# Weights of a seven-product projection: requested in another queue, split in another order

## The reference

```python
h = rms_norm(x, norm_w[l]) * (1.0 + scale[:, None, :]) + shift[:, None, :]
proj = jnp.einsum('bsd,de->bse', h, w_in[l])                      # 2888 columns
u_pool, g_pool, q, k, v, g_attn, qi, ki, wi = jnp.split(proj, split_points, axis=-1)
pool_out = pool_mixer(u_pool, w_pool[l], pool_scale[l]) * jax.nn.silu(g_pool)
q = rope(rms_norm(q.reshape(B, S, N_HEADS, HEAD_DIM), q_norm_w[l]), pos)
k = rope(rms_norm(k.reshape(B, S, N_KV_HEADS, HEAD_DIM), k_norm_w[l]), pos)
qi, ki = rope(qi...), rope(ki...)
```

## Time and profile before

| | us |
|---|---|
| median of three executions | 3118.74 (3116.83 to 3121.08) |
| the profiled execution's own time | 3112.07 |
| its span, from the first to the last instruction | 3110.3 |
| TensorE busy | 2921.1 (94%) |
| VectorE busy | 2345.5 (75%) |
| ScalarE busy | 1748.3 (56%) |
| GpSimd busy | 349.3 (11%) |
| mean granted clock of TensorE | 0.975 of full speed |

### The profile page before, as it was taken

How to read it: one execution, slowest core, us unless ns; L and a number is a source line. 1 busy time by engine, 2 the same in 40 slices (tenths; PEclk the granted TensorE clock), 3 DMA queues, 4 the chain that set the end, 5 groups by cost and what they waited for, 6 DMA issues and landing times. The chain is left out here.

```text
span 3110.3 us, 49557 instructions
## 1 busy us (share of the span) xinstructions
PE 2921.1 (94%) x17248; PEld 2331.0 (75%) x17248; DVE 2345.5 (75%) x3555; ACT 1748.3 (56%) x3207; POOL 349.3 (11%) x695
## 2 busy tenths in 40 slices
PE   7999999999999999999999998798777899999899
PEld 5888888888878877777777777577656667777687
DVE  8888887766576859888879766666568898888553
ACT  5343422232455537777767654455378899888510
POOL 2000000000000441000100000000012333233100
PEclk8999999999999999999999999999988999999999
DMA  4434422257855883210137665566661111111774
GB/s 123 123 105 130 149 68 68 68 183 263 223 150 182 272 276 88 52 32 29 46 116 225 194 189 170 187 177 186 183 140 45 25 32 29 25 39 39 166 219 140
DMA packets 449820, 401.00 MB, mean 129 GB/s; under 512 B 106563, under 2 KB 379971, under 8 KB 447141
## 3 DMA queue, kind: packets, MB, share of 16 engines
q1 hardware_dynamic: 447764, 393.58, 43.1%
q0 software_dynamic: 1088, 3.93, 0.6%
q10 hardware_dynamic: 720, 0.31, 0.1%
HBM read 263.20 MB, written 124.49 MB: 125 GB/s over the span
## 5 line engine op out<-in xcount | busy, mean ns | idle before, releaser
L349 ACT ACTIVATE s_mx_w_hi<-s_mx_raw 128x512 fp32r<-128x512 f32 x224 | 138.5, 628 | 309.3 <-PE p_oa_acc L705 238.1
L705 PE MATMUL p_oa_acc<-s_h_a_hi,s_mx_w_hi 128*128 128x512 f32 x744 | 291.6, 392 | 8.4 <-DVE s_h_a_lo L448 7.1
L705 PE MATMUL p_oa_acc<-s_h_a_hi,s_mx_w_lo 128*128 128x512 f32 x744 | 290.5, 390 | 0.0
L705 PE MATMUL p_oa_acc<-s_h_a_lo,s_mx_w_hi 128*128 128x512 f32 x744 | 290.4, 390 | 0.0
L2143 PE MATMUL p_pr_ps<-s_pr_x_hi,s_pr_w_hi 128*128 128x512 f32 x588 | 235.0, 400 | 34.4 <-ACT s_pr_first L2137 18.0
L1862 DVE TENSOR_TENSOR_SCAN s_st_prod<-s_st_soft,s_st_prod 128x512 f32<-128x512 f32 x192 | 234.9, 1270 | 8.3 <-ACT s_st_soft L1789 7.6
L2143 PE MATMUL p_pr_ps<-s_pr_x_lo,s_pr_w_hi 128*128 128x512 f32 x588 | 232.4, 395 | 0.0
L2143 PE MATMUL p_pr_ps<-s_pr_x_hi,s_pr_w_lo 128*128 128x512 f32 x588 | 232.0, 395 | 0.0
L1789 ACT ACTIVATE s_st_soft<-p_st_z 128x512 f32<-128x512 f32 (+3 forms) x320 | 153.5, 532 | 109.4 <-PE p_st_z L1915 108.5
L4313 PE MATMUL p_sa_turn<-s_ident,s_sa_arg 128*128 128x128 f32 x1088 | 165.1, 287 | 40.5 <-ACT s_sa_prob L3911 22.3
L2108 DVE TENSOR_TENSOR s_pr_w_lo<-s_pr_w_raw,s_pr_w_hi 128x512 fp32r<-128x512 f32 x154 | 105.1, 687 | 119.2 <-ACT s_pr_w_hi L2103 118.9
(11 more groups left out here) (487 smaller groups left out, 7748.8 us busy)
## 6 DMA issues: line engine op xcount, KB each, us to landing
s_mx_raw<-in_w_in_a SPq DMA_DIRECT2D x128, 256.0 KB, 3.7
s_pr_w_raw<-d_w_sums SPq DMA_DIRECT2D x88, 256.0 KB, 3.7
s_pr_w_raw<-in_w_in SPq DMA_DIRECT2D x66, 256.0 KB, 3.7
s_pb_ada<-in_w_ada SPq DMA_DIRECT2D x16, 768.0 KB, 7.3
s_pb_block<-in_w_in SPq DMA_DIRECT2D x44, 256.0 KB, 4.6
d_w_sums<-s_pb_block SPq DMA_DIRECT2D x44, 256.0 KB, 3.0
d_rot_hi<-s_pr_rot SPq DMA_DIRECT2D x18, 512.0 KB, 2.9
d_y_t<-s_mx_y SPq DMA_DIRECT2D x16, 512.0 KB, 5.5
```

Of the source, the lines that this page charges most:

```text
L349: nc.scalar.activation(w_hi[:, m], raw[g % 2][:, m], ACT.Copy).then_inc(hi_done, 1)
L705: ins = nc.tensor.matmul(bank, w[:, m, k, :], a[:, m, k, :], start=(k == 0 and n == 0), stop=(k == KH - 1 and n == 2))
```

## The change

- SyncE no longer requests weights in this stage. All its loads of weights move to GpSimd's queue, in the order in which the products free the slots. Of group 0 (the tail) and group 1 they stand in `out_b_programs.gpsimd`, of the others in `rotate_programs.gpsimd`, where `late_difference` follows the loads of the tail 12.
- SyncE's loop keeps the swaps and the stores. `store_inverse` and `spread_inverse` come earlier in it, `load_ahead` moves from before group 11 to the end of group 10, `load_late_half(0)` goes behind the swap, and `load_first_rows` and `load_first_keys` go later.
- ScalarE makes the high part of a slot about two products after the same slot was freed: A12_B21, S3_T3, S4_B22 and A22_T4 within their own group, A11_B11, S1_T1 and S2_T2 (behind `keep_u3`) in the group before. `take_high` of the norm group g - 2 comes right behind `leave`, ahead of everything else.
- VectorE's order follows: `times_inverse` first, then `low_squares` or `add_windows`, `times_sin`, the low part of A12_B21, `times_cos`, `add_turned`, S3_T3, `low_turned` of the norm group, and so on. `leave_b` now stands ahead of `low_pooled`. `leave_b` of the tail 0 moves ahead of the last splits of the stage before (`leave_tail`).

```diff
@@ -2335,26 +2335,7 @@
                 load_x(n + 2)
-            if n == RESIDENT:
-                for h in range(2):
-                    pairs.load_tail(sp, 0, h)
             if RESIDENT <= n - 4:
                 store_late(n - 4)
-            if n == TILES - 2:
-                sp.wait_ge(product, TILES - 3)
-                pairs.load(sp, FIRST, S.A11_B11)
-            if n == TILES - 1:
-                sp.wait_ge(product, TILES - 2)
-                pairs.load(sp, FIRST, S.S1_T1)
-                sp.wait_ge(product, TILES - 1)
-                pairs.load(sp, FIRST, S.S2_T2)
-                sp.wait_ge(transposed, TILES - 3)
-                pairs.load(sp, FIRST, S.S4_B22)
         store(TILES - 1)
-        sp.wait_ge(transposed, TILES - 2)
-        pairs.load(sp, FIRST, S.A22_T4)
-        for n in range(TILES - 4, TILES - 2):
-            store_late(n)
-        pairs.load(sp, FIRST, S.A12_B21)
-        for n in range(TILES - 2, TILES):
+        for n in range(TILES - 4, TILES):
             store_late(n)
-        pairs.load(sp, FIRST, S.S3_T3)
 
@@ -2362,2 +2343,17 @@
         nc.gpsimd.memset(eps, EPS).then_inc(ready, 1)
+        pool.wait_ge(product, RESIDENT)
+        for h in range(2):
+            pairs.load_tail(pool, 0, h)
+        pool.wait_ge(product, TILES - 3)
+        pairs.load(pool, FIRST, S.A11_B11)
+        pool.wait_ge(product, TILES - 2)
+        pairs.load(pool, FIRST, S.S1_T1)
+        pool.wait_ge(product, TILES - 1)
+        pairs.load(pool, FIRST, S.S2_T2)
+        pool.wait_ge(transposed, TILES - 3)
+        pairs.load(pool, FIRST, S.S4_B22)
+        pool.wait_ge(transposed, TILES - 2)
+        pairs.load(pool, FIRST, S.A22_T4)
+        pairs.load(pool, FIRST, S.A12_B21)
+        pairs.load(pool, FIRST, S.S3_T3)
 
@@ -2478,2 +2474,11 @@
 
+        def leave_tail():
+
+            dve.wait_ge(pairs.product, len(pairs.TAIL_PRODUCTS))
+            dve.wait_ge(pairs.first_kept, 1)
+            for j in range(2):
+                dve.wait_ge(xf_out[j], 16 * (TILES // 2))
+            rows = slice(0, pairs.TAIL)
+            nc.vector.tensor_tensor(pairs.upper[0][rows, PART:], pairs.bank_b(ps)[rows], pairs.first[rows], ALU.add).then_inc(pairs.b_left, 1)
+
         dve.wait_ge(norm_in, 16)
@@ -2496,2 +2501,4 @@
                 sum_up((i - 6) // 2, i % 2 == 0)
+            if i == STEPS:
+                leave_tail()
             for n in pieces_of(i - 1):
@@ -2555,3 +2562,3 @@
     groups, N = pairs.groups, len(pairs.groups)
-    LATE = N // 2
+    FIRST, LATE = 1, N // 2
     LAST = LATE - 1
@@ -2791,9 +2798,5 @@
         for g in range(N):
-            was, nxt = g - 1, g + 1
+            was = g - 1
             was_kind = kinds[was] if g else "none"
-            more = g > 0 and nxt < N and kinds[nxt] != "tail"
             norm, pool = older(g, "norm"), older(g, "pool")
-            if g == LAST:
-                load_ahead()
-                load_late_half(0)
             if g == LATE + 1:
@@ -2804,6 +2807,4 @@
                 swap(was)
-            if kinds[g] != "tail" and was_kind != "tail":
-                pairs.load(sp, g, S.A22_T4)
-            if more:
-                pairs.load(sp, nxt, S.A11_B11)
+            if g == LAST:
+                load_late_half(0)
             if norm is not None:
@@ -2817,4 +2818,2 @@
                 store_plain(was, True, lower_out[was % 2])
-            if more:
-                pairs.load(sp, nxt, S.S1_T1)
             if norm is not None:
@@ -2823,24 +2822,13 @@
                 gather_roots(was)
-            if g == N - 1:
-                load_first_keys()
+                store_inverse(was)
             if pool is not None:
                 store_rot(pool)
-            if more:
-                pairs.load(sp, nxt, S.S2_T2)
+            if was_kind == "norm":
+                spread_inverse(was)
             if pool is not None:
                 store_low(pool)
-            if was_kind == "norm":
-                store_inverse(was)
+            if g == LAST - 1:
+                load_ahead()
             if g == LAST:
                 load_late_half(1)
-                for h in range(2):
-                    pairs.load_tail(sp, nxt, h)
-            if more:
-                pairs.load(sp, nxt, S.A12_B21)
-            if was_kind == "norm":
-                spread_inverse(was)
-            if g == N - 2:
-                load_first_rows()
-            if more:
-                pairs.load(sp, nxt, S.S3_T3)
             if was_kind == "pool":
@@ -2851,6 +2839,2 @@
                 store_low(was)
-            if more:
-                pairs.load(sp, nxt, S.S4_B22)
-                if kinds[g] == "tail":
-                    pairs.load(sp, nxt, S.A22_T4)
             if g == N - 2:
@@ -2859,3 +2843,5 @@
                 sp.wait_ge(out.r1_out, 16)
+                load_first_rows()
                 load_queries(sp, space.q_two, space.q_in, 0, ROT_Q, rot_hi, rot_lo)
+        load_first_keys()
         load_queries(sp, space.qi_two, space.qi_in, FIRST_SELECTING + 1, ROT_QI, rot_hi, rot_lo)
@@ -2881,3 +2867,10 @@
         pool.wait_ge(ones_ready, 4)
-        late_difference()
+        for g in range(FIRST + 1, N):
+            if kinds[g] == "tail":
+                for h in range(2):
+                    pairs.load_tail(pool, g, h)
+                late_difference()
+                continue
+            for q in range(MULTS):
+                pairs.load(pool, g, q)
 
@@ -3010,20 +3003,20 @@
                 leave(was)
-                if was_kind == "norm":
-                    split_squares(was)
-                if was_kind != "tail":
-                    open_rest(was)
+            if norm is not None:
+                take_high(norm)
+            if was_kind == "norm":
+                split_squares(was)
+            if was_kind not in ("none", "tail"):
+                open_rest(was)
             if g == LATE:
                 late_high(3)
-            if whole:
-                pairs.split_hi(nc, act, g, S.S4_B22)
-                if g == LATE + 1:
-                    late_high(6)
-                pairs.keep_first(nc, act, ps, g)
-                pairs.split_hi(nc, act, g, S.A22_T4)
-            elif g:
+            if g == LATE + 1:
+                late_high(6)
+            if g:
                 pairs.keep_first(nc, act, ps, g)
+            if g == LATE:
                 late_high(4)
                 late_high(5)
-            if norm is not None:
-                take_high(norm)
+            if whole:
+                pairs.split_hi(nc, act, g, S.A12_B21)
+                pairs.split_hi(nc, act, g, S.S3_T3)
             if was_kind == "pool":
@@ -3036,6 +3029,12 @@
                 keep_u2(g)
+                pairs.split_hi(nc, act, g, S.S4_B22)
             if was_kind == "pool":
                 split_pooled(was)
+            if whole:
+                pairs.split_hi(nc, act, g, S.A22_T4)
             if more and g:
                 pairs.split_hi(nc, act, nxt, S.A11_B11)
+            if g == LAST:
+                late_high(0)
+                late_high(1)
             if pool is not None:
@@ -3044,4 +3043,2 @@
                 pairs.split_hi(nc, act, nxt, S.S1_T1)
-            if more:
-                pairs.split_hi(nc, act, nxt, S.S2_T2)
             if whole:
@@ -3050,14 +3047,10 @@
                 take_high(was)
-            if g == LAST:
-                late_high(0)
-                late_high(1)
+            if more:
+                pairs.split_hi(nc, act, nxt, S.S2_T2)
             if was_kind == "pool":
                 blend(was)
-            if more:
-                pairs.split_hi(nc, act, nxt, S.A12_B21)
-                pairs.split_hi(nc, act, nxt, S.S3_T3)
             if g == LAST:
+                late_high(2)
                 for h in range(2):
                     pairs.split_tail_hi(nc, act, nxt, h)
-                late_high(2)
             if kinds[g] == "norm":
@@ -3246,2 +3239,5 @@
                 late_low(2)
+                late_low(3)
+            if norm is not None:
+                times_inverse(norm)
             if g == LATE + 1:
@@ -3250,18 +3246,8 @@
                 low_squares(was)
-            if norm is not None:
-                times_inverse(norm)
             if was_kind == "pool":
                 add_windows(was)
-            if whole:
-                pairs.split_lo(nc, dve, g, S.S4_B22)
-            if g == LATE:
-                late_low(3)
             if was_kind in ("norm", "tail"):
                 times_sin(was)
-            if norm is not None:
-                low_turned(norm)
             if whole:
-                if g == LATE + 1:
-                    late_low(5)
-                pairs.split_lo(nc, dve, g, S.A22_T4)
+                pairs.split_lo(nc, dve, g, S.A12_B21)
             if was_kind in ("norm", "tail"):
@@ -3269,4 +3255,13 @@
                 add_turned(was)
+            if whole:
+                pairs.split_lo(nc, dve, g, S.S3_T3)
+                if g == LATE + 1:
```

(46 more changed lines are left out.)

14 lines of the change are left out of this document (7 added, 7 removed).

## The result

The changed kernel takes 3129.18 us (median of 6 runs, 3123.26 to 3133.7), the kernel before 3118.13 us in the same comparison (6 runs, 3112.3 to 3121.08). The ratio is 1.0035, 95% interval 1.0025 to 1.0045: slower by 0.35%, where the prediction said 35 us faster. The profiled execution took 3128.93 us with a span of 3127.1 us, 16.8 us above the span before. Granted clock 0.974.

The account below looks back on a forecast made before the run. TensorE, busy 94%, bounds the kernel, so only its waits can shrink, many behind late weight requests. 16.4 + 12.1 + 10.7 - 3.8 - 0.4 = 35.0 us gained, from 3118.7 to 3083; 8-in-10 range 3056 to 3106.

Parts of the forecast that it names:

- Requests: 154 weight requests on GpSimd's queue, 0.75 us each, blocks landing in 5.5 us (ends 3.7 and 13.2); nothing waits at 5.5.
- The slower rival: Weights land too late on GpSimd's queue and hold every whole group; 59 us in 22 groups, 3142 us; chance 9%.
- the one of descriptors in VectorE's way: Rival: GpSimd's requests delay VectorE 5.3 us per group; six norm groups wait, 18 us off the gain, 3101; chance 14%.
- Norm groups behind a pool: Eight norm groups: 20.5 us each plus 26 for waits and clock, 190 us together.
- The waits before A12_B21 and the pool product: In norm groups behind windows 16, 8 and 4: waits of 5.3, 4.0 and 2.8 us, together 22.4.
- Pool groups and their like: Groups 2, 4, 6, 8, 10, 14, 16, 18, 20, 22: all blocks in time, 20.1 us each.
- Group 1: A12_B21's low part stands behind times_sin of the tail, whose swap is late; 3.8 us lost with the slow clock.
- Groups 11 to 13: Groups 11 and 12 take 39 us against 49.7, gain 10.7 (bounds 5 and 18); group 13 loses 0.4.
- Group 23: Weights no longer stand behind load_first_rows: 20.0 us against 32.1, gain 12.1.
- no wait over 1 us: Sign expected in the profile after: TensorE has no wait over 1 us in group 23.

Follow-up runs that it names:

- e2: Kernel before with only the new orders of ScalarE and VectorE in this stage, weights and everything else requested by SyncE as before; 3113.19 us, ratio 0.9991.
- e3: Changed kernel with two SyncE lines swapped back, so the older pool's low rows are stored ahead of the spread inverse; 3121.55 us, ratio 1.0024.
- e6: Changed kernel with low rows stored ahead of the spread inverse and ScalarE's take_high of the normed rows behind keep_first again; 3128.47 us, ratio 1.0036.
- e5: Changed kernel with VectorE, in group 1 alone, doing all low parts and leave_b ahead of times_sin of the tail; 3118.08 us, ratio 1.0006.
- e10: Changed kernel with GpSimd's one large operation, the difference for S3_T3, given to VectorE in group 12; 3116.2 us, ratio 1.0007.
- e1: Kernel before with only the weight requests moved to GpSimd's queue, all orders of ScalarE, VectorE and the rest of SyncE as before; 3110.32 us, ratio 0.9983.
- e4: Changed kernel with leave_c ahead of finish in VectorE; 3122.87 us, ratio 1.0027.
- e9: Changed kernel, low rows stored ahead of spread inverse, invert ahead of add_turned, add_windows and A12_B21's low part ahead of times_inverse, take_high after u2's copy; 3120.76 us.

## Why the prediction was wrong

The sum was made of steps; here is each against the profile after, in its own terms.

*Requests: right.* 154 on GpSimd at 0.55 and 0.75 us, landing in 3.3 us in the middle against the 5.5 taken. The slower rival (blocks too late on GpSimd's queue) and the one of descriptors in VectorE's way both fall: VectorE is busy 2339.9 us in the kernel, 2345.5 before.

*Norm groups behind a pool: the step that failed.* I said "`finish`, `leave_c` and the low part of S2_T2 then end at 22.3, that is 2.2 us into the norm group", and counted their lateness only through `add_windows`. Two things were wrong in it. The size: `finish` runs near 26, since the store goes out at 19.3 and not at 16.5 (the low rows are made at 18.3, behind `leave_b`, `invert` and three low parts) and lands after 5.1 to 7.7 us and not 4.0, for I took the landing of the old order, where no 512 KB stood ahead of it. And the place: the second product waits for `leave_c`, and it is due 2.7 us into the group. I never put the time of `leave_c` beside that product. At my own 22.3 it would just have passed, which is why nothing warned me. The eight groups take 209.8 us, 19.8 over the forecast. There are 20.3 us of waits for `leave_c` in six of them (groups 11 and 23 have 3.1 and 4.2 more), and five of the six products behind such a wait took 4.3 to 5.5 us instead of 2.9, at the lower clock for part or all of it. The waits before A12_B21 and the pool product that I had priced at 22.4 us came to 9.8; TensorE was already late when it came to them, which fits, but no run separates the two.

A second term was put at nothing. The new order of ScalarE has `take_high` of the normed rows ahead of `keep_first`, and it ends only after the spread inverse has landed and `times_inverse` has run; I counted `take_high` for group 23 alone, at 0.8 us, and the landing nowhere. In e2 and e3, where the store goes ahead of the spread, the third products behind a pool and in groups 11 and 23 wait 24.0 and 22.5 us for `keep_first`, and in e6, which moves `take_high` behind it, these waits are gone. So with the store put right the forecast would still have failed: the eight groups take 201.4 us in e3, not 190.

*Pool groups and their like:* 210.4 instead of 201, most of it before the sixth product, 0.3 to 1.2 us in eight of ten groups; group 14 waits 1.6 us before the fourth. I had the low part of S4_B22 at 13 us, due at 14.5. It stands behind `times_sin`, `times_cos` and `add_turned` of the older pool, and ahead of all this VectorE stands for the swap, 29.5 us in the ten groups, a wait that my count did not have. In group 6 it is 2.7 us, and the low part ends 15.3 us into the group.

*Group 1:* forecast 3.8 us longer, 8.2 measured. The mechanism is the one named, and e5 shows it. I had the swap requested 6.6 us into the group and landed 8.5 later. It was requested at 7.8, since SyncE, as before the change, first issued cos, sin, the pool's weights and a store, and it landed 10.1 us later. Why the landing took longer stays open.

*Groups 11 to 13:* 5.4 us gained instead of 10.3. Group 11 waits for `leave_c` (3.1 us) and `keep_first` (1.8), and GpSimd's operation, which now falls on `finish` (5.07 us), holds the tail; e10 gives the last back. *Group 23:* 5.3 gained instead of 12.1, because "no wait over 1 us" left out `leave_c` once more (4.17 us and the clock). The old wait, for `keep_first`, is gone as forecast.

The differences add up: 19.8 + 9.4 + 4.4 + 4.9 + 6.8 = 45.3 us in the stage, and 6.5 around it, make the 51.8 between -35.0 and +16.8.

The rival that ended slower was about the wrong queue. I asked how late GpSimd's blocks could be and did not ask the same of what stayed with SyncE, though its order was changed too. What I said of the earlier trace rows, that time is lost to order in a queue and not to issue or transfer, holds for this store as well, and I applied it only to the requests that moved away. How much of the loss is that store's is less clear. e1 and e2 have one part each, and neither is slower, because each wins more in the other groups than it loses behind the pools. The changed kernel's stage is 15.4 us longer than that of e1, 10.6 of it in group 1, 5.9 in the even groups and only 0.8 in the odd ones. And e3, with the store back in its place, is still 0.24% slower than before and took back some 3 us of 11, so the store is at most a part of it, and e4, e6 and e9 each passed the wait on to the next thing in line.
